# Three small moves in a two-layer decoder trunk: load lines issued ahead of a store, attention biases written at other tiles, one weight's high part one tile later

## What is computed

```python
# layer 0: differential attention, 4 heads, two softmax maps per head, ALiBi, causal
s = q @ k.T * scale - slope[h] * dist;  p = softmax(where(dist >= 0, s, -inf))
a = p[map 0] - lam * p[map 1];          ya = rmsnorm(a @ v) * (1 - lambda_init)
x = x + concat([ya, pooled]) @ w_out
# layer 1: dilated attention, 8 heads of width 64; the three branches make one additive mask
s = q @ k.T * scale - slope[h] * dist + log(count of branches that hold this key)
yd = softmax(s) @ v;                    x = x + concat([conv_gate, yd]) @ w_out
# both layers
x = x + (silu(h @ w_gate) * (h @ w_up)) @ w_down          # D_FF = 2816 = 22 chunks of 128
```

## Time and profile before

| what | value |
|---|---|
| median of 3 runs | 2194.54 us (2193.26 to 2195.07) |
| the profiled execution | 2192.01 us |
| its span, first to last instruction | 2190.2 us |
| granted TensorE clock over the span | 1.000 |
| PE busy | 2152.4 us, 98% |
| DVE, ACT, POOL busy | 1321.8, 901.0, 859.3 us |
| chain that ended last | PE 80%, issue 13%, DVE 2%, ACT 2%, POOL 2%, DMA 1% |

### The profile page before, as it was taken

How to read it: one execution, slowest core, us unless ns; L and a number is a source line. 1 busy time by engine, 2 the same in 40 slices (tenths; PEclk the granted TensorE clock), 3 DMA queues, 4 the chain that set the end, 5 groups by cost and what they waited for, 6 DMA issues and landing times.

```text
span 2190.2 us, 30207 instructions
## 1 busy us (share of the span) xinstructions
PE 2152.4 (98%) x10572; PEld 1805.7 (82%) x10572; DVE 1321.8 (60%) x1829; ACT 901.0 (41%) x1497; POOL 859.3 (39%) x563
## 2 busy tenths in 40 slices
PE   8999899999999999999999999999999999999999
PEld 7877798888888887888888888988888888888887
DVE  4345875765565654558597256656865555555555
ACT  4134874443333334445332148642433333334433
POOL 1022432467666772002244033220567777651000
PEclk9999999999999999999999999999999999999999
DMA  5011321055554448675311111311255555557655
GB/s 191 6 57 44 125 78 30 20 183 199 186 201 154 158 159 288 192 240 163 116 39 51 56 58 40 117 39 39 58 193 187 186 179 168 172 167 279 196 194 192
DMA packets 229535, 295.56 MB, mean 135 GB/s; under 512 B 11824, under 2 KB 133168, under 8 KB 229168
## 3 DMA queue, kind: packets, MB, share of 16 engines
q1 hardware_dynamic: 229136, 294.04, 41.2%
q10 hardware_dynamic: 288, 0.05, 0.0%
HBM read 208.06 MB, written 77.59 MB: 130 GB/s over the span
## 4 chain that ended last, share of the span: by engine, by line
PE 80%; issue 13%; DVE 2%; ACT 2%; POOL 2%; DMA 1%; SPq 0%; POOLq 0%; DVEq 0%; ACTq 0%
PE PS L1531 12%; PE PS L1529 12%; PE PS L1530 12%; PE PS L1556 6%; PE PS L1558 6%; PE PS L1557 6%; PE PS L1181 4%; PE PS L1083 4%; PE PS L1085 4%; PE PS L1084 4%; PE PS L1162 2%; POOL QRS L989 1%; PE PS L1137 1%; PE PS L1138 1%; PE PS L1246 1%
## 5 line engine op out<-in xcount | busy, mean ns | idle before, releaser
L2134 DVE TENSOR_TENSOR LINEl<-LINE,HIGH 128x1024 fp32r<-128x1024 f32 x154 | 194.3, 1269 | 167.2 <-ACT HIGH L1587 166.6
L1587 ACT ACTIVATE HIGH<-LINE 128x1024 fp32r<-128x1024 f32 x154 | 163.1, 1060 | 235.2 <-PE PS L1558 213.4
L1556 PE MATMUL PS<-HIGH 128*128 128x512 f32 x616 | 240.3, 390 | 3.4 <-ACT KEEP L1587 3.0
L1558 PE MATMUL PS<-HIGH,LINEl 128*128 128x512 f32 x616 | 239.7, 389 | 0.0
L1557 PE MATMUL PS<-LINEl,HIGH 128*128 128x512 f32 x616 | 239.7, 389 | 0.0
L2134 DVE TENSOR_TENSOR SLOTl<-BLOCKS,RING 128x512 fp32r<-128x512 f32 x168 | 156.7, 933 | 96.8 <-ACT RING L1587 92.2
L921 POOL TENSOR_TENSOR ST<-ST 128x512 f32<-128x512 f32 x132 | 193.8, 1468 | 32.7 <-DMA ST<-in_ffn_w_down 24.1
L1587 ACT ACTIVATE RING<-BLOCKS 128x512 fp32r<-128x512 f32 x168 | 105.9, 630 | 227.2 <-PE PS L1531 216.8
L2134 DVE TENSOR_TENSOR SLOTl<-SLOT,RING 128x512 fp32r<-128x512 f32 x126 | 129.8, 1031 | 87.0 <-ACT RING L1587 86.8
L1556 PEld LDWEIGHTS PS<-HIGH 128*128 128x128 f32 x616 | 115.6, 188 | 28.4 <-issue 3.8
L989 POOL TENSOR_TENSOR QRS<-QMS,EXPO 128x8 f32<-128x8 f32 x32 | 52.1, 1640 | 220.6 <-DVE QMS L2395 220.1
(11 more groups left out here) (418 smaller groups left out, 5796.0 us busy)
## 6 DMA issues: line engine op xcount, KB each, us to landing
LINE<-hidden SPq DMA_DIRECT2D x154, 256.0 KB, 2.7
hidden<-HID SPq DMA_DIRECT2D x44, 512.0 KB, 4.3
ST<-in_ffn_w_down SPq DMA_DIRECT2D x44, 512.0 KB, 4.1
sums<-ST SPq DMA_DIRECT2D x22, 1024.0 KB, 6.2
hidden<-ST SPq DMA_DIRECT2D x22, 1024.0 KB, 6.6
LINE<-sums SPq DMA_DIRECT2D x88, 256.0 KB, 3.0
BLOCKS<-in_ffn_w_gate SPq DMA_DIRECT2D x42, 512.0 KB, 4.0
BLOCKS<-in_ffn_w_up SPq DMA_DIRECT2D x42, 512.0 KB, 5.2
```

The source lines that it names most:

```text
L1556: pe.matmul(dst, hi[:, 0, ts], hi[:, 1, :], start=j == 0 and not adds_on, stop=False, skip_group_check=adds_on)
L1558: pe.matmul(dst, lo[:, 0, ts], hi[:, 1, :], start=False, stop=j == NJ - 1, skip_group_check=adds_on).then_inc(dn_pe, 1)
L1587: return nc.scalar.activation(dst, src, ACT.Copy, **kw)
L2134: return v.tensor_tensor(dst, src, hi.bitcast(F32), ALU.subtract)
```

## The change

It has three parts that don't touch each other. In SP's program the store of the last sums stands behind line 13 and no longer behind line 10. In layer 1's attention, units use BX and BIAS by turns; unit 1's pair is written at n = 4 and n = 5 (no wait is needed, since BIAS is free), and the pair of unit u + 2 is written at the end of tile i = 7 of unit u, both biases one behind the other, behind `turned(1)`. ACT makes WO3h at n = 31 and no longer at n = 30.

```diff
--- before.py
+++ after.py
@@ -840,10 +840,10 @@
                 store_hidden(FC - 1, 1, True)
                 store_duty(FC - 2, True)
                 load_duty(FC - 1, True)
-                for s in range(8, 11):
+                for s in range(8, 14):
                     load_step(s)
                 store_duty(FC - 1, True)
-                for s in range(11, STEPS):
+                for s in range(14, STEPS):
                     if L == 0 and s == 50:
                         load_v(1, 0)
                         load_v(1, 1)
@@ -1924,7 +1924,7 @@
                         elif n == 27:
                             act.wait_ge(stack_lo, stacks_before(0, 3))
                             high_w("q3", QWh3[:], QWs[3][:])
-                        elif n == 30:
+                        elif n == TILES0 - 1:
                             for m in range(2):
                                 act.wait_ge(s_pe[m][0], TILES0)
                             high_w("g3", WO3h[:], WO3s[:])
@@ -2418,7 +2418,11 @@
                 att = Tally(dve, att_seq[L])
 
                 def bias(m, b, hd):
-                    out = BIAS[m if L else b] if hd > L else BX[hd]
+                    if L == 0:
+                        out = BIAS[b] if hd else BX[0]
+                    else:
+
+                        out = (BX, BIAS)[b][m]
                     att.did(v.scalar_tensor_tensor(out=out[:], in0=DIST[:], scalar=SM[:, hd + 8 * L:hd + 8 * L + 1],
                                                    in1=MASK[:], op0=ALU.mult, op1=ALU.add))
 
@@ -2431,10 +2435,10 @@
                         dve.wait_ge(t_pe[0][0], g + i + 1)
                     u, t = (g + i) // NT, (g + i) % NT
                     keys, c = P * (t + 1), m + 2 * (t % 2)
-                    if u == 0:
-                        table = BX[m if L else 0]
+                    if L == 0:
+                        table = BIAS[u % 2] if u else BX[0]
                     else:
-                        table = BIAS[m if L else u % 2]
+                        table = (BX, BIAS)[u % 2][m]
                     v.tensor_tensor_reduce(out=PR[m][t % 2][:, 0:keys], in0=PS[:, 1024 * m:1024 * m + keys], in1=table[:, P * (7 - t):TOK],
                                            scale=-1.0, scalar=3.0e38, op0=ALU.add, op1=ALU.min,
                                            accum_out=NMX[:, c:c + 1]).then_inc(s_mx[m][L], 1)
@@ -2575,8 +2579,12 @@
                         b, g, more = u % 2, NT * u, n + 1 < TILES0
 
                         def next_bias(m):
-                            dve.wait_ge(s_mx[m][1], g + 9)
-                            bias(m, 1 - b, 2 * u + 2 + m)
+
+                            if i == NT - 1:
+                                dve.wait_ge(s_mx[m][1], g + 9)
+                                bias(m, b, 2 * u + 4 + m)
+                            else:
+                                bias(m, 1, 2 + m)
 
 
                         if n > 0:
@@ -2592,12 +2600,15 @@
                         if more:
                             biased(1, b, g, i + 1)
                         turned(0, n)
-                        if i == NT - 2 and u + 1 < UNITS:
+                        if n == 4:
                             next_bias(0)
                         if n > 0:
                             scaled(0, n - 1)
                         turned(1, n)
-                        if i == NT - 2 and u + 1 < UNITS:
+                        if n == 5:
+                            next_bias(1)
+                        elif i == NT - 1 and u + 2 < UNITS:
+                            next_bias(0)
                             next_bias(1)
                     denominator(0, TILES0 - 1)
                     scaled(1, TILES0 - 2)
```

## The result

| what | before | after |
|---|---|---|
| median | 2194.98 us (21 runs, 2191.68 to 2199.73) | 2200.28 us (21 runs, 2194.27 to 2203.07) |
| ratio after / before, 95% interval | | 1.0019 [1.0012, 1.0026] |
| the profiled execution, its clock | 2192.01 us, 1.000 | 2201.78 us, 0.993 |
| granted clock, mean of a run, over the runs | 0.996 to 1.000 | 0.992 to 0.996 |

The account below looks back on a forecast made before the run. PE was taken as the bound, busy 2152.4 of 2190.2 us, so its idle time was counted: -1.3 + 2.35 (biases) - 1.9 = -0.85 us, giving 2193.7 us on the median; range 2189.8 to 2197.0, about 8 in 10.

Parts of the forecast that it names:

- WO3h at n = 31: End of layer 0's attention: PT's copy starts at 342.27, not 343.58, so PE starts earlier; -1.3 us, bounds -1.58 and 0.
- biases taken from tile 6: Layer 1's attention: `scaled(0, 5)` no longer waits for a bias; -0.85 us three times, -2.55.
- the pairs: End of tile 7, units 0 and 1: PE's 128x384 score waits 1.95 us for two biases, twice; +3.9 us.
- the bias at n = 5: Layer 1's attention, ahead of `biased` of tile 7: it delays PE's next score; +0.4 us.
- the bias at n = 4: Layer 1's attention: slowed beside POOL, it delays `scaled(0, 3)`; +0.6 us taken, from +0.15 to +1.15.
- the store behind line 13: Step 11 of the down products: gains of 0.7 us in layer 0, 1.2 in layer 1; -1.9, bounds -3.0 and +1.1.
- T: Landing time of the last sums' store, which `down_hi(11)` needs; up to 864.8 gives the whole 1.57 us, 866.4 nothing.
- The second rival: Store lands late in both layers, T at 867.0: the step gives +0.6 + 0.5, sum +2.15, 2196.7 us; chance 0.14.
- The 0.1 for refilling the pipeline: Layer 1's attention: about 0.1 us of pipeline refilling goes with each 0.75 us stop of PE that is removed.
- the lower bound: Bias at n = 4: slowed beside POOL, it ends at 1331.8 at best, costing +0.15 us.
- The full +1.15: Bias at n = 4: it gets nothing until POOL is done and ends at 1332.8, costing +1.15 us.

Follow-up runs that it names:

- the first experiments: The first four kernels timed together beside before (2195.08 us): biases alone, the other two parts, biases spread, PE kept busy in the long stops.

## Why the prediction was wrong

The prediction's sum was of PE's idle time, and there it was right in direction and place, and 2 us off in size. Step by step:

| step | forecast, us | measured in PE's idle time |
|---|---|---|
| WO3h at n = 31 | -1.3 | 1.58 to 0.28: -1.3 |
| biases taken from tile 6 | -2.55 | -2.25 |
| the pairs | +3.9 | 2 x 1.71: +3.4 |
| the bias at n = 5 | +0.4 | +0.24 |
| the bias at n = 4 | +0.6 | none in brackets (0.15 by the start, see below) |
| the store behind line 13 | -1.9 | -3.0 |
| sum | -0.85 | -2.9 |
| the granted clock | not a term | PE's busy time +13.1 |

**The step that failed** is the pair's: "PE thus stands for 2.4 - 0.45 = 1.95 us, twice: +3.9", with bounds of 0.7 and 2.6 each. The stop had the right place, releaser and length. It was costed at its own length, as if the products behind it went on at full speed. In the trace of the changed kernel they run at 1.2 GHz for about 14 and 10 us, and the biases' part costs +9.9 us by its ratio where +2.35 was forecast. The kernel with these stops filled shows that the standing still does it, and puts its price at 8.3 us. In the profile of the one with a single bias, a stop of 0.52 there did not bring it. No rival had the clock in it, and the range ended at the counted bounds.

The hint lay in the prediction's own base. It noted that the profiled execution stood 2.5 us below the median, and took both at a clock of 1.000. The runs of before beside the first experiments say what lies between them: those at a clock of 0.999 or 1.000 took 2191.2 to 2194.4 us, those at 0.996 to 0.998 took 2194.8 to 2200.5. Before itself loses some clock in most of its executions; its profile happened to be one that did not. So the base was a lucky execution, in the clock and in the short waits at the steps 11.

**The store** was mis-sized even in idle time: T, when it has landed, was taken as 865.7. It was 862.24, or 863.5 on before's scale, where all is 1.3 later. I let the three lines' transfers start at 856.2 and the store queue behind them. But SP issued them by 854.43, while it would have waited for POOL anyway; the store went out 0.03 us after POOL's sums, as in before, and landed 5.3 later, against 5.2 in the earlier trace rows. Three more lines ahead cost it nothing that shows. The second rival, a late store, is refuted.

**Two smaller terms.** The 0.1 for refilling the pipeline, added to each 0.75, is shown by no run: the stops that went were 3 x 0.75. And the bounds given for the biases' sum, -1.5 and +3.5, are not those of its terms, which add up to -0.6 and +4.2.

**What held.** PT's copy was forecast for 342.3 and stood at 342.31; WO3h lay beside PE's work. The bias at n = 4 was slowed beside POOL, to 1.73 from 1.28, and ended at 1328.77, which on before's scale is the 1331.8 of the lower bound. PE's products behind it start 0.33 us after the last score and not 0.18 as in before, which is the +0.15 of that bound. They have no bracket. The full +1.15 would have needed the bias to wait until POOL was done, and POOL was busy until 1329.37. Its two pieces took 2.40 us there and 1.60 in the earlier trace rows, so POOL was slowed as well. The bias of 1340.32 spoke against the full bound already: it ended 1.08 us behind POOL's end, and alone a bias takes 1.27.

## What to carry to other kernels

Where PE is busy 98% of the time, a new stop of a microsecond or two may cost several times its length, since the clock can halve behind it. So cost an edit by its stops and, as a second term with a range of its own, by what the clock does behind them; look at PEclk over several executions, not in the one profile that happens to be at 1.000. Work for another engine that has to be done somewhere is best put one piece at a time into different tiles: the six biases make no stop of PE when spread out, and the kernel with two pairs of them is 14.5 us slower by the ratios.

## What the runs showed that was not expected

- In the changed kernel the clock stays at 1.2 GHz from 1349 to 1361 with PE busy all the time, so it isn't regained as soon as work is there.
- The two stops of 0.54 at the end of layer 1's attention, which every kernel has but the one that fills them, are followed by a low stretch in six of the ten profiles (window 1440 to 1480 at 0.91 in the changed kernel), and by none in before's. The same stops in the same order thus cost nothing or about 3.5 us, by execution. What decides it was not settled.
- The clock is also low at about 222 to 226 us, at the start of layer 0's attention, in five of the eleven profiles, and in none of before's or the changed kernel's, although every kernel has the same instructions there. One profile can't price what the clock does.
- Filling a wait of PE with products that nobody reads makes the kernel faster: by 8.3 us in the changed kernel.
